# Setup of a two-block transformer kernel: modulation rows by column halves on TensorE, squares by token, operands scaled ahead

## The reference, cut to what matters

```
c_act = silu(c)                                  # c: (1, 1024)
mod = c_act @ w_ada + b_ada                      # w_ada: (1024, 6144); six parts of 1024
sh1, sc1, g1, sh2, sc2, g2 = split(mod, 6)
h = rms_norm(x, pre_mix_g) * (1.0 + sc1) + sh1   # x: (1024 tokens, 1024)
proj = h @ w_in                                  # then mLSTM, attention, w_out, FFN, second block
```

## Time and profile before

| what | value |
|---|---|
| device time, 3 runs | 2281.47 us median (2278.68 to 2282.75) |
| profiled execution | 2280.47 us, its span 2278.7 us |
| PE busy | 96% of the span, 10080 matmuls; weight loads 78% |
| DVE, ACT, POOL busy | 71%, 49%, 35% |
| DMA | 332.35 MB, mean 146 GB/s |
| granted TensorE clock, mean | 0.99 of full speed |

### The profile page before, as it was taken

One profiled execution on the slowest core, in us unless ns is written; L12 is line 12 of the kernel. 1 busy time (PEld: TensorE's weight loads), 2 busy tenths in 40 slices (PEclk: granted clock), 3 DMA queues, 4 the chain that ended last, 5 costly groups with the idle time before them and its releaser, 6 DMA issues.

```text
span 2278.7 us, 28954 instructions
## 1 busy us (share of the span) xinstructions
PE 2191.4 (96%) x10080; PEld 1778.8 (78%) x10080; DVE 1615.0 (71%) x2191; ACT 1122.2 (49%) x1916; POOL 793.3 (35%) x578
## 2 busy tenths in 40 slices
PE   6999998998899999999998999999999999999999
PEld 5888886686688888888876767777778888888887
DVE  6658357727999999985797579993675555556686
ACT  5652257736554444455455578872343333334533
POOL 1120044424623232342022536661364343433310
PEclk9999999999999999999999999999999999999999
DMA  9356532033133232299854230003423333338986
GB/s 353 99 182 221 179 93 65 28 111 130 55 103 120 89 119 90 93 317 387 311 166 141 68 102 20 28 0 130 130 70 102 107 102 107 102 120 318 368 280 230
DMA packets 282782, 332.35 MB, mean 146 GB/s; under 512 B 18626, under 2 KB 180754, under 8 KB 282138
## 3 DMA queue, kind: packets, MB, share of 16 engines
q1 hardware_dynamic: 279976, 323.10, 41.9%
q0 software_dynamic: 2208, 7.37, 0.9%
q10 hardware_dynamic: 465, 0.17, 0.0%
HBM read 251.90 MB, written 79.73 MB: 146 GB/s over the span
## 4 chain that ended last, share of the span: by engine, by line
PE 54%; DVE 9%; POOL 6%; DMA 4%; issue 3%; ACT 3%; SPq 1%; POOLq 0%; DVEq 0%; ACTq 0%
PE ps L2698 11%; PE ps L2699 11%; PE ps L2700 11%; POOL cbuf L1786 4%; DMA shared<-ffn_blocks 3%; PE ps L2724 3%; PE ps L2725 3%; PE ps L2726 3%; PE ps L358 1%; PE ps L360 1%; PE ps L359 1%; DVE wlo L2904 1%; PE ps L326 1%; DVE sum_lo L2907 1%; PE ps L327 1%
## 5 line engine op out<-in xcount | busy, mean ns | idle before, releaser
L2698 PE MATMUL ps<-sum_hi,whi 128*128 128x512 f32 x640 | 249.7, 390 | 1.8 <-DVE cbuf L3419 0.9
L2700 PE MATMUL ps<-sum_hi,wlo 128*128 128x512 f32 x640 | 249.0, 389 | 0.0
L2699 PE MATMUL ps<-sum_lo,whi 128*128 128x512 f32 x640 | 249.0, 389 | 0.0
L2724 PE MATMUL ps<-sum_lo,whi 128*128 128x512 f32 x616 | 240.7, 391 | 0.8 <-ACT arena L2809 0.8
L2726 PE MATMUL ps<-sum_lo,wlo 128*128 128x512 f32 x616 | 239.7, 389 | 0.0
L2725 PE MATMUL ps<-sum_lo,whi 128*128 128x512 f32 x616 | 239.7, 389 | 0.0
L2698 PE MATMUL ps<-hhi,whi 128*128 128x512 f32 x480 | 188.1, 392 | 7.8 <-DVE cbuf L3374 3.3
L2700 PE MATMUL ps<-hhi,wlo 128*128 128x512 f32 x480 | 187.7, 391 | 0.0
L2699 PE MATMUL ps<-hlo,whi 128*128 128x512 f32 x480 | 187.7, 391 | 0.0
L1786 POOL TENSOR_TENSOR cbuf<-cbuf,attn_stats 128x1024 f32<-128x1024 f32 x80 | 151.7, 1896 | 88.2 <-DVE attn_stats L2048 88.2
L796 POOL TENSOR_TENSOR cbuf<-cbuf 128x512 f32<-128x512 f32 (+1 forms) x50 | 77.3, 1548 | 300.8 <-ACT cbuf L783 298.3
(11 more groups left out here) (455 smaller groups left out, 5573.9 us busy)
## 6 DMA issues: line engine op xcount, KB each, us to landing
shared<-ffn_blocks SPq DMA_DIRECT2D x154, 256.0 KB, 5.0
lead_work<-in_w_down SPq DMA_DIRECT2D x105, 256.0 KB, 4.4
arena<-in_w_down SPq DMA_DIRECT2D x100, 256.0 KB, 3.8
raw<-in_w_up SPq DMA_DIRECT2D x36, 512.0 KB, 4.8
ffn_blocks<-chunk_work SPq DMA_DIRECT2D x66, 256.0 KB, 2.3
ffn_blocks<-lead_work SPq DMA_DIRECT2D x66, 256.0 KB, 2.3
raw<-in_w_in SPq DMA_DIRECT2D x32, 512.0 KB, 4.7
arena<-in_w_ada SPq DMA_DIRECT2D x32, 512.0 KB, 5.7
```

Of the source, the lines that this page charges most:

```text
L2698: nc.tensor.matmul(o, hi[:, ws], mhi, start=fresh and k == 0, stop=False, skip_group_check=True)
L2699: nc.tensor.matmul(o, hi[:, ws], mlo, start=False, stop=False, skip_group_check=True)
L2700: mm = nc.tensor.matmul(o, lo[:, ws], mhi, start=False, stop=(k == 3), skip_group_check=True)
L2724: nc.tensor.matmul(o, hi[:, ws], mhi, start=fresh, stop=False, skip_group_check=True)
```

## The change

It computes the same values in another way:

- A modulation row is no longer 1024 columns of one part. `half_rows(n)` takes 512 columns of sh1 and the same 512 of sc1. Rows 0 to 7 give both parts for feature tiles 0 to 3 (half 0), rows 8 to 15 for tiles 4 to 7 (half 1).
- `multiply_ada` lets PE multiply a row with one column of c_act and add up over rows in PSUM. Rows 0 to 7 are multiplied in setup, 8 to 10 at the start of the next block, 11 and 12 behind the products of k = 0 and 1. Rows 13 to 15 stay with DVE and are reduced by PE ahead of k = 4.
- Squares are taken with tokens on partitions, as x was loaded, and summed along the row by ACT. The root per token is spread onto a diagonal by DVE, and PE turns it into rows with two matmuls against ones.
- Tiles 0 to 3 of x are multiplied by the root in setup (`x_unit`); their operands then need only gain and shift.
- SP's order: weight tiles 0 and 1 go between rows 3 and 4; rows 14 and 15 wait until x is turned and squared; weight tiles 2, 3 and the gate columns move into the next block, ahead of the parking of xt. The three small loads are issued by POOL.
- The sigmoid of c is built from Exp, an addition and a reciprocal, so that one table load of ACT goes.

```diff
+        def half_rows(n):
+            h, k = n // DK, n % DK
+            return a["w_ada"][0][k * P:(k + 1) * P, 0:2 * D].rearrange("p (s c) -> p s c", s=2)[:, :, h * HALF:(h + 1) * HALF]
+        def multiply_ada(pe, n):
+            sums = mod_sums[n // DK]
+            if n % DK == 0:
+                nc.tensor.matmul(sums, onesF[:, :], zeros, start=True, stop=False)
+            pe.wait_ge(s_ada[n], 16)
+            for j in range(DK):
+                mm = nc.tensor.matmul(sums[:, j:j + 1], ada_slots[n][:, j * P:(j + 1) * P], csil[:, n % DK:n % DK + 1],
+                                      start=False, stop=(n == DK - 1 and j == DK - 1))
+            mm.then_inc(ada_multiplied, 1)
...
# FirstNorm.pe, in place of pair_products
+                for n in range(DK, DK + 3):
+                    multiply_ada(pe, n)
...
+                for k in range(DK):
+                    if k == 4:
+                        pe.wait_ge(ada_added, DK * 2 - ADA_PE)
+                        for j in range(DK):
+                            mm = nc.tensor.matmul(mod_sums[1][:, j:j + 1], ada_acc[:, j * P:(j + 1) * P],
+                                                  onesF[:, 0:1], start=False, stop=(j == DK - 1))
+                        mm.then_inc(ada_reduced, 1)
+                    pe.wait_ge(self.op_lo, k + 1)
...
+                    if k < ADA_PE - DK - 3:
+                        multiply_ada(pe, DK + 3 + k)
# FirstNorm.dve
+                for k in range(4):
+                    value(k)
+                    low(k)
+                    if k >= 1:
+                        add_row(ADA_PE + k - 1)
+                dve.wait_ge(ada_reduced, 1)
+                modulate_half(1).then_inc(mod_ready, 1)
+                dve.wait_ge(mod_ready, 1)
+                gains_half(1).then_inc(mod_ready, 1)
+                dve.wait_ge(mod_ready, 2)
+                for k in range(4, DK + 1):
                     if k < DK:
+                        value(k)
+                    if k > 4:
+                        low(k - 1)
...
# setup, SP
+                for n in range(2 * DK):
+                    if n == 4:
+                        for w in range(RAW):
+                            load(sp, At(w), tile_source(At(w)))
+                    if n == 2 * DK - 2:
+                        sp.wait_ge(x_turned, DK)
+                        sp.wait_ge(x_squared, NB)
+                    sp.dma_start(ada_slots[n].rearrange("p (s c) -> p s c", s=2), half_rows(n)).then_inc(s_ada[n], 16)
# setup, PE
+                for b in range(2):
+                    pe.wait_ge(s_x[b], 16)
+                    for k in range(3):
+                        turn(k, range(4 * b, 4 * b + 4))
+                pe.wait_ge(sums_zero, 1)
+                pe.wait_ge(c_sig, 2)
+                multiply_ada(pe, 0)
+                pe.wait_ge(x_copied, 1)
+                turn(3, range(NB))
+                multiply_ada(pe, 1)
...
+                mm.then_inc(par_turned, 1)
+                pe.wait_ge(x_copied, 2)
+                turn(4, range(NB))
+                multiply_ada(pe, 2)
+                pe.wait_ge(x_copied, 4)
+                pe.wait_ge(rstd_spread, 1)
+                for hf in range(2):
+                    mm = nc.tensor.matmul(rstd_sums[:, half(hf)], onesF[:, :], rstd_blocks[:, half(hf)], start=True, stop=True)
+                mm.then_inc(x_summed, 1)
+                turn(5, range(NB))
+                multiply_ada(pe, 3)
+                pe.wait_ge(x_copied_late, 1)
+                turn(6, range(NB))
+                multiply_ada(pe, 4)
+                pe.wait_ge(x_copied_late, 2)
+                turn(7, range(NB))
+                for n in range(5, DK):
+                    multiply_ada(pe, n)
# setup, ACT
+                for b in range(NB):
+                    act.wait_ge(s_x[b // 4], 16)
+                    if b:
+                        act.wait_ge(x_squared, b)
+                    nc.scalar.activation(square_out, xin[:, b, :], ACT.Square, accum_out=square_sums[:, b:b + 1])\
+                      .then_inc(x_squared, 1)
...
# setup, DVE
+                dve.wait_ge(s_small, 16 * 3)
+                nc.vector.tensor_scalar(sinks, sinks_in, -1.0, None, ALU.mult).then_inc(sinks_scaled, 1)
+                for k in range(4):
+                    dve.wait_ge(x_turned, k + 1)
+                    nc.vector.tensor_copy(xt[:, k, :], turned_to[k][:, :]).then_inc(x_copied, 1)
...
+                for k in range(4):
...
+                    nc.vector.tensor_tensor(x_unit[:, k, :], xt[:, k, :], rstd_sums, ALU.mult).then_inc(x_scaled, 1)
...
+                dve.wait_ge(ada_multiplied, DK)
+                ch.link(modulate_half(0))
+                ch.step(gains_half(0))
```

More of the change, by code:

```diff
@@ L378, in reduce_ada @@
             return mm
[L380 to L399, removed]
         xt = ar(0, DK, T)
         xin = ar(32, NB, D)
-        ada_acc = [ar(64, D), chunk_work[:, 7 * D:8 * D]]
-        ada_slots = [cbuf[:, i, :] for i in range(2)] + [chunk_work[:, i * D:(i + 1) * D] for i in range(7)]
-        ada_slots += [v[:, i * D:(i + 1) * D] for v in (row_hi, row_lo) for i in (2, 3)]
+        ada_acc = ar(64, D)
+        ada_slots = [chunk_work[:, i * D:(i + 1) * D] for i in range(DK)] + [cbuf[:, i, :] for i in range(2)]
+        ada_slots += [v[:, i * D:(i + 1) * D] for v in (row_hi, row_lo) for i in (2, 3)] + [xin[:, i, :] for i in range(2)]
         c_in = lead_work[0:DK, 7 * T:7 * T + P]
-        c_turned = up[1][:, 0:DK]
+        mod_sums, params_out = [down[1][:, 0:DK], down[0][:, 0:DK]], down[1][:, HALF:HALF + 384]
+        zeros = small[:, 56:64]
+        c_turned = down[1][:, T - DK:T]
         par_in = ar(68, 3, P)
@@ L449, in coef_col @@
             return coef[:, 8 * c + k:8 * c + k + 1]
[L452 to L469, removed]
-            def sp(self, sp):
[L472 to L481, removed]
-            def act(self, act):
[L484 to L493, removed]
@@ L501, in act @@
                     ins.then_inc(self.op_hi, 1)
[L502 to L512, removed]
@@ L514, in dve @@
-            def dve(self, dve):
[L515 to L530, removed]
-                    if k < DK:
[L532 to L550, removed]
@@ new lines, in _ @@
+                pe.wait_ge(sums_zero, 1)
[4 more added lines that the diff above has]
+                multiply_ada(pe, 1)
+                pe.wait_ge(s_par, 16 * n_par)
+                for c in range(3):
+                    mm = nc.tensor.transpose(params_out[:, c * P:(c + 1) * P], par_in[:, c, :], identF[:, :])
+                mm.then_inc(par_turned, 1)
+                pe.wait_ge(x_copied, 2)
@@ L669, in _ @@
                 act.sem_inc(up_free, 2)
+                nc.scalar.preload_act_table_set(LN_EXP)
                 act.wait_ge(c_done, 1)
[L671 to L676 removed]
@@ L677, in _ @@
-                for k in range(DK):
-                    act.wait_ge(x_turned, k + 1)
-                    nc.scalar.activation(xt[:, k, :], down[k % 2][:, :], ACT.Copy).then_inc(x_copied, 1)
-                    act.wait_ge(x_copied, k + 1)
-                    nc.scalar.activation(squares[:, k, :], xt[:, k, :], ACT.Square).then_inc(x_squared, 1)
-                for w in range(AHEAD):
-                    split_hi(act, At(w))
-                act.wait_ge(x_summed, 1)
-                norm_mix.act_rstd(act, 0)
+                nc.scalar.activation(csig, c_turned, ACT.Exp, scale=-1.0).then_inc(c_sig, 1)
```

207 lines of the change are left out of this document (123 added, 84 removed).

## The result

| what | before | after |
|---|---|---|
| device time, 6 runs each | 2282.77 us median (2278.68 to 2283.68) | 2311.74 us median (2304.50 to 2318.45) |
| ratio to before, 95% interval | 1 | 1.0129 (1.0116 to 1.0142) |
| profiled execution, its span | 2280.47, 2278.7 us | 2318.45, 2316.7 us |
| matmuls | 10080 | 10248 |
| gate products begin | 70.17 us | 103.85 us |

The changed kernel is 29 us slower. That is the predicted 2312.0 to 0.3 us, but the agreement of the medians is closer than the steps deserve, as the comparison further down shows.

What follows compares the result with a forecast made beforehand. PE, busy 96%, bounds the kernel; its summed order, with narrow work at half clock, put gate products at 101.5 against 70.17 us. These 31.3 us on 2280.47 gave 2311.8, median 2312.5; likeliest case's range 2304 to 2320, stated range 2285 to 2319.

Steps and rivals of the forecast that it cites:

- one `multiply_ada`, half clock / full: On PE: eight one-column matmuls for a modulation row, priced like a reduction, 3.41 us at half clock, 1.71 at full.
- end of row 0's group: PE in setup: transposes from 14.57 to 17.1, zeros 0.4, row 0's multiplication 3.41 at half clock, ending at 21.0 us.
- stall ahead of k = 4: PE waits after reducing rows 13 to 15 for modulation, gains and DVE's values 4, 5 and low 4: 4.35 us.
- the work itself: On PE: 13 row multiplications added, seven sums and one reduction removed, net 8.8 us more work.
- spell of full clock after the root matmuls: PE in setup: 5.1 us of wide work to 36.9 brings the clock up, assumed to last 3.4 us.
- The row of 131.91: Earlier trace, 131.91 to 134.87: PE never idle with 40 narrow matmuls, then clock 0.50; taken as narrow matmuls costing the clock.
- m3: PE's `multiply_ada` of row 3 in setup, right after the root matmuls and a turn: 1.71 us at full clock.
- m4: PE's `multiply_ada` of row 4 in setup, near the end of the full-clock spell: 2.4 us, done at 41.9.
- What I priced at nothing: DVE's, ACT's, POOL's and SP's changes and the DMA order, all off PE's path: 0 us.
- POOL's three small loads: Setup: issued from 8.4 us, landing by about 17; PE needs DVE's copy queued behind them at 20 or later: nothing.
- (A): Rival: PE's clock is lost only to idling, not narrow matmuls; 5.8 to 7.7 us later, 2288.5 us; chance 0.27.
- (B): Rival, faster: a `multiply_ada` on PE is cheaper than the reduction, at half 0.85 us; 2276 to 2278 us; chance 0.07.

Runs made afterwards that it cites:

- one-column version: The changed kernel with seven of the eight matmuls of every `multiply_ada` left out, so most modulation values are wrong: 2283.19 us median of 10 runs, ratio 1.0003.

## Why the prediction was right, step by step

| step | predicted | measured | with x at 14.57 |
|---|---|---|---|
| one `multiply_ada`, half clock / full | 3.41 / 1.71 | 3.41 / 1.71 | |
| end of row 0's group | 21.0 | 22.3 | 20.9 |
| first product | 65.5 | 66.79 | 65.3 |
| stall ahead of k = 4 | 4.35 | 4.35 | |
| first product of k = 4 | 88.2 | 90.07 | 88.6 |
| gate products | 101.5 | 103.85 | 102.4 |

The last column takes off the 1.45 us by which x came later.

**Work and clock.** The 33.7 us between the gate products before and after divide so. At half clock PE was busy from 16.02 to about 37.8 (the turn at 36.56 is between both speeds), 30.0 us from 41.3 to 72.1, and 5.9 us behind the stall; half of each is lost, 10.9 + 15.0 + 2.9 = 28.8 us. Before, the same sum is 2.7 (14.57 to 19.9, as the sums at 19.54 still took 2.08 us for 1.88) + 2.2 = 4.9. So 23.9 us of the 33.7 are the clock, 1.45 are x, 0.3 is idle time, and what is left, 8.1, is the work itself, which was predicted as 8.8. That narrow groups cost the clock is shown twice, by putting them where nothing else changed and by keeping the clock with wide work between them.

**Where I chose, and was lucky.** The spell of full clock after the root matmuls was a guess from one row of before. The row of 131.91 was itself weaker than the prediction says: its 40 records are 32 transposes and four matmuls of two records each, so it was the later run that showed the effect for one-column matmuls. In the profiled run the spell began and ended within a microsecond of where I put it (m3 at full clock, m4 half of each). In the version with rows behind products, whose work up to there is the same, the clock was up in the first group, half from 21.0 to 31.2, and up until 41.5. So this step is right in kind, and its place is chance. I take the 14 us between the fastest and slowest of the six runs to be of this kind too, but the clock's places in the other five were not traced.

**What I priced at nothing.** Copies, spread, squares (finished at 20.9, "by 21") and SP's holding back rows 14 and 15 cost nothing, as the one-column version shows as a whole. POOL's three small loads did cost: I asked only when they land, and not what they do to a 2 MB load under way. That is 1.45 us, the one step ahead of the gate products that failed; 0.9 us more are sizes, most of it the half clock behind the stall (5.9 us for 5.1).

**The end of the sum.** I added the time behind the gate products unchanged. In the profiled run the total grew by 38.0 us and not 33.7: 2214.6 us lie behind the gate products, against 2210.3 before. It is 2212.4 in the one-column version, 2211.0 to 2217.8 in the other versions. In the changed kernel the 4.3 us are the clock: the same 9853 records keep PE busy 2143.7 us there against 2139.2 before, with as much idle time, and spells of half clock of 3 to 10 us fall at other places. The medians agree with 2312 because the profiled run was the slowest of the six (2318.45 against the 2311.8 that the sum gives for it), and the step from 2311.8 to the median, 1.0 us, makes 2312.8 and not the 2312.5 of the prediction; a prediction from this trace's own order of time to better than about 5 us would be a claim too much.

**The rivals.** (A) fell on the 64 one-column records at 170.00. (B) fell on every group: 1.71 us at full clock in open sums as in closed ones, never 0.85.

## What to carry to other kernels

Before work is moved onto the busiest engine, count it there in its real unit (8 one-column matmuls with 128 x 128 weights: 1.71 us, as long as 7.5 products of 512 columns), and ask what it does to the clock of all that stands around it: 8.1 us of work came with 23.9 us lost to the half clock. Put such groups one at a time between wide products. What made the same idea pay, by 0.27%, was to leave the rows on the engine with time to spare, to put one narrow group where PE idles anyway, and to start the reduction one product earlier, so that the chain behind it has cover.

## What the runs showed that I had not expected

- One-column matmuls with full 128-row weights and no idle time brought the clock from 2.4 to 1.2 GHz 4.4 us after they began (170.0 to 174.4), and it came back 5 us after wide products ran again. At 216.51 it took 2.3 us, at 261.48 5.1 us.
- Behind a stall of 4.35 us the clock was at 0.50 in the change and in each version that has it; in the version with rows behind products it had fallen before, at 68.8. Behind one of 1.46 us it was not. Each of the long stalls follows directly on a narrow reduction, and the two were not taken apart.
- Transposes raised the clock, in some executions: in the version with rows behind products the first group behind two runs of 12 of them (at 9.14 and 14.57), at 17.47, already took 1.97 us and not 3.4; with the same transposes it took 3.55 in the version with the small loads last. The Trainium skill (TensorE: Matmul & The Clock Gate, "Part 4: PE-mode transpose") says that they do not; for these float32 transposes the trace disagrees.
- Three small loads issued by POOL beside a 2 MB load took the DMA rate to 124 GB/s where it had been 390 to 405, and delayed that load by 1.45 us.
- The granted clock of a trace is shown as 1.00 until the first fall in it, also where the durations of matmuls are doubled (here up to 37.8).
